# State-space outputs: lag products and most state copies inside the scan, eight state slots, one scan step fewer

## The reference, cut to what matters

```python
def s5_layer(u, ...):
    a_bar = jnp.exp(lam * dt)                                    # complex, 64 states
    ug = u.reshape(b, s, N_GROUPS, SSM_GROUP)                    # 64 groups of 16 features
    def scan_dir(u_row, r, reverse):
        bu = jnp.einsum('sgh,gph->sgp', u_row, b_bar[r])
        _, states = lax.associative_scan(_ssm_combine, (a, bu), reverse=reverse, axis=0)
        return jnp.einsum('sgp,ghp->sgh', states, c_mat[r]).real
    y = scan_dir(.., 0, False) + scan_dir(.., 1, True)
    y = y.reshape(b, s, D_MODEL) + d_skip * u
    g = jax.nn.gelu(y)
    val, gate = jnp.split(g @ w_glu, 2, axis=-1)
    return val * jax.nn.sigmoid(gate)
```

## Time and profile before

| what | value |
|---|---|
| time, median of 3 runs | 1937.5 us (1935.07 to 1937.52) |
| the profiled execution | 1932.74 us, its span 1931.0 us |
| PE busy | 1815.3 us (94% of the span) |
| DVE busy | 1297.0 us (67%) |
| ACT busy | 782.1 us (41%) |
| mean granted TensorE clock | 0.978 of full speed |
| chain that ended last | PE 83%, DVE 10%, ACT 4% |

### The profile page before, as it was taken

How to read it: one execution, slowest core, us unless ns; L and a number is a source line. 1 busy time by engine, 2 the same in 40 slices (tenths; PEclk the granted TensorE clock), 3 DMA queues, 4 the chain that set the end, 5 groups by cost and what they waited for, 6 DMA issues and landing times.

```text
span 1931.0 us, 25968 instructions
## 1 busy us (share of the span) xinstructions
PE 1815.3 (94%) x9518; PEld 1476.3 (76%) x9518; DVE 1297.0 (67%) x2455; ACT 782.1 (41%) x1259; POOL 39.1 (2%) x35
## 2 busy tenths in 40 slices
PE   7997999999999981999999999899999989999898
PEld 6785578888888851888888788789787778888786
DVE  4856866866886679435655687459888767676365
ACT  5226854422342361425321332334776353333111
POOL 0000000000000000000000000000132000000000
PEclk9999999999999995999999999999999999999999
DMA  6320012455545489333444676223101222223422
GB/s 205 107 95 18 1 35 84 133 158 154 169 152 160 142 244 130 130 100 120 145 159 136 205 231 221 66 88 110 33 23 45 66 77 98 98 89 107 159 94 75
DMA packets 99930, 225.02 MB, mean 117 GB/s; under 512 B 19296, under 2 KB 48608, under 8 KB 99824
## 3 DMA queue, kind: packets, MB, share of 16 engines
q1 hardware_dynamic: 53520, 166.81, 28.3%
q10 hardware_dynamic: 46304, 56.77, 9.5%
HBM read 202.68 MB, written 20.87 MB: 116 GB/s over the span
## 4 chain that ended last, share of the span: by engine, by line
PE 83%; DVE 10%; ACT 4%; issue 2%; ACTq 1%; DMA 0%; DVEq 0%; SPq 0%
PE PS L432 25%; PE PS L434 24%; PE PS L433 24%; PE PS L961 1%; DVE ST L2023 1%; DVE mx L1822 1%; PE PS L625 1%; PE PS L607 1%; DVE WL L1551 1%; PE PS L945 1%; DVE Sst L2027 1%; DVE Sst L2030 1%; DVE Ca L2115 1%; PE PS L540 1%; PE PS L953 1%
## 5 line engine op out<-in xcount | busy, mean ns | idle before, releaser
L1551 DVE TENSOR_TENSOR WL<-raw,WH 128x1024 fp32r<-128x1024 f32 x228 | 277.2, 1221 | 304.7 <-ACT WH L1045 294.4
L1045 ACT CAST WH<-raw 128x1024 fp32r<-128x1024 f32 x228 | 237.4, 1046 | 518.1 <-PE PS L434 451.4
L432 PE MATMUL PS<-XH,WH 128*128 128x512 f32 x928 | 366.4, 395 | 5.6 <-DVE XL L1585 5.4
L434 PE MATMUL PS<-XH,WL 128*128 128x512 f32 x928 | 362.4, 390 | 0.0
L433 PE MATMUL PS<-XL,WH 128*128 128x512 f32 x928 | 362.3, 390 | 0.0
L432 PE MATMUL PS<-WH,AH 128*128 128x512 f32 x688 | 270.6, 393 | 5.4 <-DVE AL L2318 5.4
L434 PE MATMUL PS<-WH,AL 128*128 128x512 f32 x688 | 268.6, 390 | 0.0
L433 PE MATMUL PS<-WL,AH 128*128 128x512 f32 x688 | 268.5, 390 | 0.0
L432 PE MATMUL PS<-WH,XH 128*128 128x512 f32 (+2 forms) x512 | 198.3, 387 | 14.9 <-DVE XL L1621 10.4
L432 PEld LDWEIGHTS PS<-XH,WH 128*128 128x128 f32 x928 | 175.0, 189 | 43.8 <-DVE XL L1585 6.1
L434 PEld LDWEIGHTS PS<-XH,WL 128*128 128x128 f32 x928 | 174.9, 188 | 37.2
(11 more groups left out here) (356 smaller groups left out, 2480.4 us busy)
## 6 DMA issues: line engine op xcount, KB each, us to landing
raw<-units_dram SPq DMA_DIRECT2D x272, 512.0 KB, 3.3
ada_late<-ada_units_dram ACTq DMA_DIRECT2D x48, 512.0 KB, 4.3
wi_scratch<-WIe ACTq DMA_DIRECT2D x16, 512.0 KB, 2.8
ca_scratch<-CAr ACTq DMA_DIRECT2D x32, 256.0 KB, 3.5
WI<-wi_scratch SPq DMA_DIRECT2D x16, 512.0 KB, 8.9
CA<-ca_scratch SPq DMA_DIRECT2D x16, 512.0 KB, 5.2
Tm<-k_scratch SPq DMA_DIRECT2D x8, 512.0 KB, 19.7
bc<-bc_dram ACTq DMA_DIRECT2D x16, 160.0 KB, 2.2
```

Source lines behind the costliest of these rows:

```text
L432: pe.matmul(o, lh, rh, start=start, stop=False)
L434: return pe.matmul(o, ll, rh, start=False, stop=stop)
L1045: nc.scalar.copy(WH[:, (u + n) % SLOTS], raw[:, s]).then_inc(hi_done, 1)
L1551: v.tensor_tensor(WL[:, s], raw[:, (u + n) % 2], WH[:, s].bitcast(F32), ALU.subtract).then_inc(unit_ready, 1)
```

## The change

- The last scan step (position 63) is left out: no output reads that state. `scan_first` and `scan_all` are each one step lower.
- `H2` has eight slots instead of four (16 KB instead of 8 KB, over the place of `WI`). Its two zero borders are set for all slots by two memsets behind the first 20 scan steps, instead of eight memsets before the scan.
- ACT copies chunk positions 0 to 47 (`PRE` = 48) of blocks 0 to 7 during the scan, once step 47 is done, and only the remaining 15 positions after it. A dummy gelu ahead of them loads the activation table.
- PE computes the lag products of all eight outputs in eight PSUM banks (`y_bank(n) = n`) inside the scan, once step 49 is done (`WARM` = 13 steps before the end) and the loads of `Tm` have landed; `outputs` keeps only the state products.
- `GL` moves from behind `H2` to the place of `Tm`.
- Each half of the first gated chunk (feature tiles 0 to 3, then 4 to 7) now follows its four outputs, in `gated_half`: first the two tiles that the first gelu transposes gave, by token tile, then the two others. The gate goes to banks 0 to 3 and the value to banks 4 to 7, the other way round than before, up to the first two feature tiles of the second MLP.
- `gelu_lo(0)` and `gelu_lo(1)` stand inside the last 20 scan steps, behind the 15th (`TURN_AT` = 14).

```diff
+PRE, WARM, TURN_AT = 48, 13, 14
-        H2 = at("H2", R + 64 * KB, [P, 4, NCH, 2, BG])
+        H2 = at("H2", R + 64 * KB, [P, 8, NCH, 2, BG])
-        GL = at("GL", R + 72 * KB, [P, KD, SEQ], F32R)
+        GL = at("GL", R, [P, KD, SEQ], F32R)
-        scan_first, scan_all = 2 * (NCH - 1) - 1, 2 * (NCH - 1) + 2 * LAG
+        scan_pre, scan_first, scan_all = 2 * (PRE - 1) - 1, 2 * (NCH - 2) - 1, 2 * (NCH - 2) + 2 * LAG
-        g_bank = lambda k: 2 * (k % 2) + k // 2 % 2
+        g_bank = lambda k: k // 4 * 4 + 2 * (k % 2) + k // 2 % 2
+        y_bank = lambda n: n
...
+                def lags(n):
+                    q, i = n // 4, n % 4
+                    for p in range(BG):
+                        for s in range(2):
+                            g = BG * (8 * q + 4 * s + i) + p
+                            pe.matmul(psum(y_bank(n))[64 * s:64 * s + 64, p * P:(p + 1) * P], UG[:, g, :], Tm[:, g, :], start=(p == 0), stop=False)
...
+                def gated_half(q):
+                    u0 = UNITS["glu"] + 2 * q
+                    for half in range(2):
+                        for t in range(NT):
+                            if t == 0 or t == 2 and not half:
+                                pe.wait_ge(t_g.lo, t_g.base + 4 * q + (4 if half or t else 2))
+                            for v in range(2):
+                                if t == 0 and not half:
+                                    pe.wait_ge(unit_ready, u0 + v + 1)
+                                k, w = 4 * q + 2 * v + half, slice(half * 512, (half + 1) * 512)
+                                m = three(psum(t), XH[:, k, t * P:(t + 1) * P], GL[:, k, t * P:(t + 1) * P],
+                                          WH[:, (u0 + v) % SLOTS, w], WL[:, (u0 + v) % SLOTS, w], k == 0, k == KD - 1)
+                                if half and t == NT - 1:
+                                    m.then_inc(unit_used, 1)
...
                 pe.wait_ge(ssm_in, 16 * 4 + 16 * CHUNK)
...
+                pe.wait_ge(sc_b, scan_first - 2 * WARM)
+                for n in range(8):
+                    lags(n)
+                for q in range(2):
+                    for n in range(4 * q, 4 * q + 3):
+                        outputs(n)
+                    gelu_turned(q, 0)
+                    outputs(4 * q + 3)
+                    gelu_turned(q, 1)
+                    gated_half(q)
...
+                nc.scalar.activation(ew[:, 0, :], eps_rms[:, :], ACT.Gelu_apprx_tanh)
+                a.wait_ge(sc_b, scan_pre)
+                for n in range(4):
+                    states(n, 0, PRE, False)
+                a.wait_ge(sc_b, scan_first)
+                a.wait_ge(h2_zero, 2)
                 for q in range(2):
+                    if q:
+                        a.wait_ge(y_done, 4)
+                        a.wait_ge(sc_b, scan_all)
                     for n in range(4 * q, 4 * q + 4):
-                        states(n)
-                        if n > 4 * q:
+                        states(n, 0 if q else PRE)
+                        if n == 4 * q + 1:
                             gelu(n - 1)
-                        if n == 4 * q + 3:
-                            gelu_hi(4 * q)
-                            gelu_hi(4 * q + 1)
+                    gelu(4 * q + 1)
+                    gelu(4 * q + 2)
+                    gelu_hi(4 * q)
+                    gelu_hi(4 * q + 1)
                     gelu(4 * q + 3)
-                    for n in (4 * q + 2, 4 * q + 3):
-                        gelu_hi(n)
+                    gelu_hi(4 * q + 2)
+                    gelu_hi(4 * q + 3)
...
-                for s in range(4):
-                    v.memset(H2[0:64, s, 0], 0.0).then_inc(h2_zero, 1)
-                    v.memset(H2[64:P, s, NCH - 1], 0.0).then_inc(h2_zero, 1)
...
-                for i in range(LAG + 1, NCH):
-                    scan([(i, 0, 8), (i - LAG, 8, 8)])
-                for i in range(NCH, NCH + LAG):
-                    scan([(i - LAG, 8, 4), (i - LAG, 12, 4)])
+                v.memset(H2[0:64, :, 0], 0.0).then_inc(h2_zero, 1)
+                v.memset(H2[64:P, :, NCH - 1], 0.0).then_inc(h2_zero, 1)
+                for i in range(LAG + 1, NCH - 1):
+                    scan([(i, 0, 8), (i - LAG, 8, 8)])
+                for i in range(NCH - 1, NCH - 1 + LAG):
+                    scan([(i - LAG, 8, 4), (i - LAG, 12, 4)])
+                    if i == NCH - 1 + TURN_AT:
+                        gelu_lo(0)
+                        gelu_lo(1)
...
-                gelu_lo(0)
-                gelu_lo(1)
-                states(4)
                 gelu_lo(2)
                 gelu_lo(3)
-                for n in range(5, 8):
+                for n in range(4, 8):
                     states(n)
```

More of the change, by code:

```diff
@@ L645, in mlp @@
                     pe.wait_ge(rows, 6)
[L646 removed]
+                    entry(t_ffn[layer], u0, rows, 8, 4 * (1 - layer), 4 * layer)
                     def beside(k):
@@ L773, in outputs @@
                         pe.wait_ge(ca_in[(2 * n + s) % 6], ca_turn(2 * n + s))
-                    if q:
-                        pe.wait_ge(t_g.lo, t_g.base + 4)
                     for p in range(BG):
[L777 to L780, removed]
                         for ri in range(2):
                             for s in range(2):
-                                m = pe.matmul(o[s], H2[:, (2 * n + s) % 4, :, ri, p], CA[(2 * n + s) % 6][:, ri, p, :], start=False, stop=(ri == 1))
+                                m = pe.matmul(psum(y_bank(n))[64 * s:64 * s + 64, p * P:(p + 1) * P], H2[:, 4 * s + i, :, ri, p],
+                                              CA[(2 * n + s) % 6][:, ri, p, :], start=False, stop=(ri == 1 and p == BG - 1))
                     m.then_inc(y_done, 1)
@@ L798, in _ @@
                 pe.wait_ge(ev_s[0], s_evicted(NB - 1))
[L799 to L809, removed]
+                pe.wait_ge(sc_b, scan_first - 2 * WARM)
[8 more added lines that the diff above has]
+                    gated_half(q)
+                pe.wait_ge(t_g.lo, t_g.base + KD)
                 for c in range(1, 4):
@@ L814, in _ @@
                         pe.wait_ge(glu_mul, NT)
-                    token_chunk(UNITS["glu"] + 4 * c, 4 * (1 - c % 2), XH, GL, last=4 if c == 3 else None)
+                    token_chunk(UNITS["glu"] + 4 * c, 4 * (c % 2), XH, GL, last=4 if c == 3 else None)
                 pe.wait_ge(glu_add, 4)
@@ L1254, in half @@
                                 a.wait_ge(norm_sq, 2 * NT * (2 + 2 * layer))
-                            nc.scalar.activation(tmp[:, f % 2, :], psum(f % 4), ACT.Relu).then_inc(up_relu, 1)
+                            nc.scalar.activation(tmp[:, f % 2, :], psum(4 + f if layer and first and f < 2 else f % 4), ACT.Relu).then_inc(up_relu, 1)
                             a.wait_ge(up_relu, 32 * layer + n + 1)
@@ L1297, in _, with states @@
                             nc.scalar.copy(dst[64:P][:, ::-1], ps[64:P]).then_inc(ev_s[0], 1)
[L1299 to L1307, removed]
+                def states(n, first=0, last=NCH - 1, ready=True):
                     for s in range(2):
                         b = 8 * (n // 4) + 4 * s + n % 4
[L1310 to L1312 removed]
+                        src = Sst[b // 8][:, b % 8].rearrange("p c r g -> p c (r g)")
+                        dst = H2[:, b % 8].rearrange("p c r g -> p c (r g)")
+                        m = nc.scalar.copy(dst[0:64, first + 1:last + 1], src[0:64, first:last])
+                        if ready:
+                            m.then_inc(h2_ready[0], 1)
                         if n < 4:
[L1314 removed]
+                            m = nc.scalar.copy(dst[64:P, NCH - 1 - last:NCH - 1 - first][:, ::-1], src[64:P, first:last])
+                            if ready:
+                                m.then_inc(h2_ready[0], 1)
                 def gelu(n):
```

32 lines of the change are left out of this document (14 added, 18 removed).

## The result

The changed kernel takes **1923.6 us** (median of 4 runs, 1921.5 to 1924.8) against 1937.5 us (1935.1 to 1940.9) of the kernel before, measured beside it: ratio 0.9931, 95% interval [0.9917, 0.9944]. The profiled execution of the changed kernel took 1924.76 us, with a span of 1923.0 us at a mean granted clock of 0.980.

The account below looks back on a forecast made before the run. The scan on DVE bounds the stage until 764.6, then PE with ACT and DVE handing to each other. The terms put the second chunk at 810.8 against 825.07; 14.2 us off the median 1937.5 gives 1923.3, range 1920.0 to 1927.5.

Parts of the forecast that it names:

- Bound and mechanism: Scan on DVE bounds the stage until 764.6, then PE with ACT and DVE; lag products move inside the scan.
- The forecast's check: Cross-check of the sum: 7.5 us of lag products leave the path, 0.9 from the scan, less waiting and crawling in the product.
- `Tm`, not `WARM`: Lag products on PE start when `Tm` lands at 757.4, not at 751.4 where `WARM` would start them.
- that case: `Tm` in time for 751.4: PE idle from 760.3 to 765.1, and outputs might start at the lower clock level.
- The scan's end: On DVE: blocks 0 to 7 scanned at 763.7, 0.9 us earlier, and the whole scan ending at 779.7.
- the first gated half: On PE: after waiting for `gelu_lo` 2 and 3 until 781.0, the other 36 matmuls end at 789.2.
- the first rival: The clock falls in the first gated half, costing 1.5 to 2.4 us: 1925.3 us; chance 0.20.
- Output 7's CA: CA loads for output 7 start at 791.1 and land by 796.5; the output ends at 798.0.
- The second rival: DVE is held inside the scan, or CA comes late, costing 1 to 3 us: 1924.3 to 1926.3; chance 0.15.
- Behind the second chunk: From the second gated chunk's start on, PE is fed without a gap and every distance stays as before.
- The 14.2: Predicted gain in us at the second gated chunk's start: 810.8 against 825.07.

Follow-up runs that it names:

- lags_back: The changed kernel with the lag products put back inside the outputs; 1929.8 us, ratio to before 0.9962.
- tm_half: The changed kernel loading only half of `Tm`, with outputs 4 to 7 using the same half again; 1920.8 us, ratio to before 0.9912.
- step_only: The kernel before with only the last scan step left out; 1936.3 us, ratio to before 0.9998.
- after_again: The changed kernel measured once more with nothing edited; 1924.4 us, ratio to before 0.9931.
- turn_all: The changed kernel with `gelu_lo` 2 and 3 also inside the scan, two steps behind 0 and 1; 1922.6 us, ratio to before 0.9926.
- both: turn_all plus four more CA slots, loaded behind the lag products into the upper half of `Tm`'s place; 1922.5 us, ratio to before 0.9925.

## Why the prediction was right, and where it was not

The forecast was 1923.3 and 14.2 us less; measured are 1923.6 and 13.9. By the stage, though, the profile shows 10.0. Each step, with the predicted points less 691.82 and the measured ones less 694.28:

| point | predicted | measured | off |
|---|---|---|---|
| first late state copy | 71.9 | 73.1 | +1.2 |
| `Tm` landed, lag products start | 65.6 | 65.1 | -0.5 |
| lag products end | 74.8 | 73.6 | -1.2 |
| first state product | 74.8 | 74.4 | -0.4 |
| `gelu_hi` 1 ends | 82.4 | 82.5 | +0.1 |
| gated product starts | 85.6 | 85.6 | 0.0 |
| `gelu_lo` 2 there, PE goes on | 89.2 | 90.4 | +1.2 |
| first gated half ends | 97.4 | 100.4 | +3.0 |
| output 7 ends | 106.2 | 110.6 | +4.4 |
| second chunk | 119.0 | 123.3 | +4.3 |

- **Bound and mechanism: right.** Lag products inside the scan are the main part. Alone they are worth 5.4 us (lags_back). The forecast's check had 7.5 us of records leaving the path; that the other 2 us are met again by work that then follows sooner is argued, not shown.
- **`Tm`, not `WARM`: right**, and it weighs more than I gave it. Predicted start 65.6, measured 65.1 on a wait named "DMA Tm<-k_scratch"; the rate of 117 GB/s is near the 105 of rows 5. That the short pieces make it slow isn't isolated: a load of `Tm` also fills 16 partitions (`Tm[SG * j:SG * (j + 1)]`) and one of CA all 128, and no run changes one without the other. The Trainium skill (DMA: Bandwidth & Descriptors, Specifications) would have had it in time for `WARM`. The trace after disagrees again with its 117 GB/s, and tm_half shows what that case looks like: a start at 59.9, an idle gap of 3.70 us and the low clock, just as the prediction drew it. What it did not draw is that this case is no slower than the forecast one; its median is some 3 us lower, at the edge of what the intervals can tell. `Tm`'s landing swings from 65 to 69 us, and from about 66 on it delays the outputs.
- **The scan's end: 1.2 us late.** 1.05 of it lies ahead of the scan. In the state-input stage the clock was at 0.50 from 693.9 to 700.7, before from 691.8 to 695.2, and the scan started 18.5 us after UG instead of 17.5. The profiles of the kernel before and of six edited kernels show 17.5 to 17.7, those of the other four with the same code there 18.5, so this is not of the change. The memset pair takes 0.3 us (727.34 to 727.66) and puts off the 8+8 steps by 0.2 (14.85 us from the first scan step to the first of them, before 14.65), where I took 0.25, and the step is worth 0.94 on DVE (step_only).
- **The term that failed in size: the first gated half.** It was to take 8.2 us from the end of PE's wait, as 36 matmuls at the upper clock. It took 10.0, since the clock fell at 786.1, 1.4 us after PE had gone back to work behind waits of 0.70 and 1.80 us, and came back at 789.4: about 1.6 us. That is the first rival, at 0.20 and 1.5 to 2.4 us, inside the profiled execution. after_again, the same kernel, doesn't have it, and no profile of the kernels edited from it has it either, so the schedule alone doesn't bring it. The Trainium skill (TensorE: Matmul & The Clock Gate, HAM oscillation) ties a fall to a stretch without matmuls that is longer than any wait in this half; the trace disagrees, as in rows 8.
- **Output 7's CA: 1 us late.** In the prediction the loads were to land 0.3 us behind the transposes, which its sum then left out (transposes to 796.2, output 7 to 798.0). In the kernel after they were issued at 796.9 and 797.3, when output 4 was done, and the second landed 5.4 us later; PE waited 0.93. The second rival named it. What the wait costs is open: after_again has none and the same stage.
- **Behind the second chunk: right.** 1105.9 us before, 1105.4 after.

**Why the number is right all the same** is only partly shown. The 14.2 was 4 too much for the stage of the profiled executions (123.3 and 123.4 in the two of the kernel after). The medians give those 4 us back. What lies outside the stage differs between profiles of nearly the same code from 1798 to 1803 us, and the profile of before has the lowest of all. Its execution was 4.8 us below its median, the one of after 1.2 above. So the profiled pair understates the gain.

Where before's profile is fast can be read from step_only, which is the kernel before but for one scan step and whose profiled execution (1937.16 us) lies at before's median. Its stage is as long (133.6 against 133.3 us), but it reaches UG 3.7 us later (695.49 against 691.82, which is the earliest of all the profiles), in code that is the same. 1.1 us of that is there at the start of PE's work at 58.38 and 59.44 us, and 2.5 more have come by 68 us. The start with the wait ahead of it (timeline of PE) and a window behind it (columns as in rows 1), before first, then step_only:

```profile
58.38 0.50 PE L432 MATMUL PS<-WH,XH 128*128 128x512 f32 x1 [1.53 <-DVE U L1802]
60.00:62.00 2.00, 2.00 (x11) 1.64 (x10) 1.97 (x5) 0.00 (x0) 0.00 (x0) 1.00 0.71 190
```

```profile
59.44 0.79 PE L432 MATMUL PS<-WH,XH 128*128 128x512 f32 x1 [3.61 <-DVE U L1802]
60.00:62.00 2.00, 2.00 (x6) 1.58 (x5) 2.00 (x4) 0.77 (x2) 0.00 (x0) 0.50 0.39 92
```

Before's profiled execution kept its clock there and step_only's did not. Against step_only the span of the kernel after is 12.3 us shorter, 10.3 in the stage, 1.2 ahead of it and 0.8 behind it. How the rest of the 13.9, and the stage of after's other executions, divide stays open. Setting the sum against the median, which the prediction did on purpose, was the right choice, and with terms 4 us too large for the stage it was partly luck.

No version was found that beats the changed kernel beyond the spread. turn_all and both lie 1 to 2 us below it, with intervals that overlap; tm_half leaves out half of `Tm` and is no full computation.

## What to carry to other kernels

- A block of matmuls that needs nothing from a serial stage belongs beside it. Here it was worth 5.4 us, and where it ended less than 1 us before the dependent work (0.74 us in the kernel after) PE entered that at the upper clock; with a gap of 3.70 us (tm_half) it did not.
- Before you move a load forward on a shared queue, count what the loads behind it pay. Here loads that are slow per byte held up all of them: a hoped-for gain of 1.5 to 3.5 us became a loss of 43.
- Short waits in a chain where engines hand to each other are not a list of costs. Here 2.2 us of waiting behind longer state copies could be added with no measurable effect, and a wait of 0.9 us for CA was there in one execution and not in the next of the same kernel, with the same stage.
- One profiled pair doesn't give the size of a small gain. Look for a profile of an execution at the median, even of a near variant, and see where it differs.

## What the hardware showed that was not expected

- Two 512 KB loads of different shape on one queue, in turn, took 8.0 to 9.15 us a pair. WI's median landing time went from 9.5 to 25.4 us, and the engine that issues them was itself held for 8 us at an issue (714.27, 8.32 us).
- The clock rose 2.8 us after the start of the same records in one kernel and 4.3 us in another whose start was only 0.7 us earlier in the stage. So the 0.7 us by which step_only brought its outputs forward were lost again.
- In the kernel after it fell at 786.1 with matmuls running back to back since 784.67, so what PE did just before the fall doesn't explain it alone; the waits of 0.70 and 1.80 us before are what stands there.
